# Opening of a two-block transformer kernel: a new order of VectorE's and ScalarE's work, with weight splits and their fetches moved

## The reference

```python
# 1. the modulation of block 1: six rows of 1024 from one conditioning vector
mod_x = silu(c) @ mod_w + mod_b             # 48 tiles of 128 outputs, 1024 inputs each
sh1, sc1, g1, sh2, sc2, g2 = split(mod_x, 6)
# 2. the pooling mixer of block 1, its residual and its norm
hx = x * (1 + sc1) + sh1
p  = [centred_window_mean(hx_g, w) - hx_g  for g, w in enumerate((2, 4, 8, 16))]
ox = einsum('blgc,gcd->blgd', p, pool_w) * pool_scale
x  = layer_norm(2**0.25 * x + g1 * ox)      # its input to the feed-forward: x * (1 + sc2) + sh2
# 3. the long filters of block 2's Hyena mixer, and their spectra
h  = sin(freq * (sin(freq * (sin(...)) @ fw2 + fb2)) @ fw3 + fb3) @ fw_out
k_f = rfft(two_sided_kernel(h_fwd * decay, h_bwd * decay))
```

## Time and profile before

| | us |
| --- | --- |
| median of 3 runs | 1805.95 |
| lowest, highest | 1804.77, 1806.22 |
| the profiled execution | 1806.09 |
| span of its profile | 1804.8 |

### The profile page before, as it was taken

One profiled execution on the slowest core, in us unless ns is written; L12 is line 12 of the kernel. 1 busy time (PEld: TensorE's weight loads), 2 busy tenths in 40 slices (PEclk: granted clock), 3 DMA queues, 4 the chain that ended last, 5 costly groups with the idle time before them and its releaser, 6 DMA issues.

```text
span 1804.8 us, 19463 instructions
## 1 busy us (share of the span) xinstructions
PE 1755.3 (97%) x7744; PEld 1399.1 (78%) x7744; DVE 950.4 (53%) x1360; ACT 621.2 (34%) x879; POOL 701.1 (39%) x321
## 2 busy tenths in 40 slices
PE   8999999999999999999999999999999999999996
PEld 4456888888887667788888888788888788888885
DVE  8787433321365875664444213687785754444124
ACT  2524222221244554243333213532233533333222
POOL 2112444444433021334444444365553344444442
PEclk9999999999999999999999999999999999999998
DMA  9873422332221020223223222522223233322321
GB/s 360 299 282 117 138 96 94 98 101 94 94 84 62 10 70 24 82 76 100 94 96 103 94 94 93 187 94 88 87 94 109 78 94 99 100 94 93 104 95 71
DMA packets 54538, 195.76 MB, mean 108 GB/s; under 512 B 6188, under 2 KB 7406, under 8 KB 52590
## 3 DMA queue, kind: packets, MB, share of 16 engines
q1 hardware_dynamic: 52781, 188.37, 31.0%
q10 hardware_dynamic: 1666, 6.14, 1.0%
HBM read 181.90 MB, written 12.58 MB: 108 GB/s over the span
## 4 chain that ended last, share of the span: by engine, by line
PE 84%; DVE 10%; POOL 2%; issue 2%; ACT 1%; DMA 1%; SPq 0%; DVEq 0%; ACTq 0%; POOLq 0%
PE ps L518 25%; PE ps L520 25%; PE ps L519 25%; PE ps L545 2%; PE ps L574 1%; PE ps L549 1%; DVE mod_ring L1775 1%; POOL w_lo L1610 1%; DVE softmax_stats L2144 1%; DVE filter_taps L1839 1%; PE ps L677 1%; DMA mod_ring<-in_mod_t 1%; PE ps L696 1%; PE ps L561 1%; PE ps L684 0%
## 5 line engine op out<-in xcount | busy, mean ns | idle before, releaser
L1610 POOL TENSOR_TENSOR w_lo<-w_raw,w_hi 128x1024 fp32r<-128x1024 f32 (+1 forms) x234 | 570.4, 2439 | 815.3 <-ACT w_hi L1119 740.4
L1119 ACT ACTIVATE w_hi<-w_raw 128x1024 fp32r<-128x1024 f32 (+1 forms) x238 | 251.3, 1056 | 791.7 <-PE ps L520 760.3
L518 PE MATMUL ps<-act_hi,w_hi 128*128 128x512 f32 x1240 | 485.9, 392 | 5.7 <-DVE x_residual L1861 3.0
L520 PE MATMUL ps<-act_hi,w_lo 128*128 128x512 f32 x1240 | 483.2, 390 | 0.0
L519 PE MATMUL ps<-act_lo,w_hi 128*128 128x512 f32 x1240 | 483.0, 390 | 0.0
L518 PEld LDWEIGHTS ps<-act_hi,w_hi 128*128 128x128 f32 x1240 | 233.0, 188 | 55.4 <-DVE x_residual L1861 3.4
L520 PEld LDWEIGHTS ps<-act_hi,w_lo 128*128 128x128 f32 x1240 | 233.0, 188 | 48.8
L519 PEld LDWEIGHTS ps<-act_lo,w_hi 128*128 128x128 f32 x1240 | 233.1, 188 | 48.5 <-issue 0.7
L518 PE MATMUL ps<-f_hidden_hi,w_hi 128*128 128x512 f32 x528 | 208.2, 394 | 0.0
L520 PE MATMUL ps<-f_hidden_hi,w_lo 128*128 128x512 f32 x528 | 207.4, 393 | 0.0
L519 PE MATMUL ps<-f_hidden_lo,w_hi 128*128 128x512 f32 x528 | 205.6, 389 | 0.0
(11 more groups left out here) (307 smaller groups left out, 2470.4 us busy)
## 6 DMA issues: line engine op xcount, KB each, us to landing
w_raw<-in_w_stream SPq DMA_DIRECT2D x250, 512.0 KB, 3.4
mod_ring<-in_mod_t SPq DMA_DIRECT2D x18, 512.0 KB, 11.4
x_tokens<-in_mod_t SPq DMA_DIRECT2D x18, 512.0 KB, 9.6
spectra<-filter_spectra SPq DMA_DIRECT2D x16, 512.0 KB, 8.3
hy_filter<-spectra SPq DMA_DIRECT2D x8, 1024.0 KB, 4.8
mod_ring_more<-in_mod_t SPq DMA_DIRECT2D x12, 512.0 KB, 11.5
x_residual<-in_xT ACTq DMA_DIRECT2D x8, 256.0 KB, 11.8
x_tokens<-in_x_tokens SPq DMA_DIRECT2D x1, 2048.0 KB, 13.3
```

Source lines behind the costliest of these rows:

```text
L518: PE.matmul(o, lh, rh, start=start, stop=False, **kw)
L520: return PE.matmul(o, ll, rh, start=False, stop=stop, **kw)
L1119: SC.activation(B.weights(c)[0][:, 0:n], B.WR[:, c % 2, 0:n], ACT.Copy).then_inc(S.w_hi, 1)
L1610: GP.tensor_tensor(low[:, 0:n], B.WR[:, c % 2, 0:n], f32(high[:, 0:n]), ALU.subtract).then_inc(S.w_lo, 1)
```

## The change

TensorE's order stays. The four others get new orders in the opening:

- **SyncE** fetches all nine first modulation tiles ahead of weight chunk 0, and chunk 1 only behind the stores of unit 0's spectrum.
- **ScalarE** splits chunk 1 behind `copies(0)` and takes `copies(2)` ahead of `pool_in`; the copies of unit 3 are laced into `pool_in` where those of unit 2 were, and the scaling of the residual stands behind them. In the norm the squares and the copies of unit 6 are laced anew.
- **VectorE** takes decays and butterflies earlier and row sums later, cuts the pooled tiles into pairs, moves `butterfly(6)` into the sums of squares, and row sums 37 to 39 behind them (`difference_low` is the same subtraction under a name).
- **GpSimd** takes the low parts at other points, by other semaphores.

```diff
@@ ScalarE, scalar_program.start @@
         w_hi(0)
+        copies(0)
         w_hi(1)
-        copies(0)
         copies(1)
+        copies(2)
         SC.wait_ge(S.x_in, 16 * KD)
         SC.wait_ge(S.affine, 1)
         SC.wait_ge(S.fw_sums, 2)
-        pool_in(0, 2)
-        even_part(2, 0)
-        pool_in(2, 4)
-        even_part(2, 1)
-        pool_in(4, KD)
-        plus_part(2, 0)
-        plus_part(2, 1)
+        pool_in(0, 3)
+        even_part(3, 0)
+        pool_in(3, 5)
+        even_part(3, 1)
+        pool_in(5, KD)
+        plus_part(3, 0)
+        plus_part(3, 1)
         for k in range(KD):
             SC.activation(X[:, k, :], X[:, k, :], ACT.Copy, scale=ALPHA_1).then_inc(S.x_scaled, 1)
-        copies(3)
...
-        even_part(6, 0)
         SC.wait_ge(S.decayed, 32)
         w_hi(4)
+        first_square(0)
+        even_part(6, 0)
+        first_square(1)
+        first_square(2)
         even_part(6, 1)
-        first_square(0)
-        first_square(1)
+        first_square(3)
+        first_square(4)
         plus_part(6, 0)
-        first_square(2)
-        first_square(3)
+        first_square(5)
         plus_part(6, 1)
-        for k in range(4, KD):
-            first_square(k)
+        first_square(6)
+        first_square(7)
@@ GpSimd, gpsimd_program.start @@
-        GP.wait_ge(S.mod_used, 5)
+        GP.wait_ge(S.mod_used, 9)
         w_lo(0)
-        GP.wait_ge(S.mod_used, 11)
+        GP.wait_ge(S.mod_used, 13)
         w_lo(1)
...
-        GP.wait_ge(S.mod_used, 31)
+        GP.wait_ge(S.diff_lo, 8)
         w_lo(2)
-        GP.wait_ge(S.mod_used, 37)
+        GP.wait_ge(S.mod_used, 32)
         w_lo(3)
-        GP.wait_ge(S.mod_used, 40)
+        GP.wait_ge(S.ln_centred, 1)
         w_lo(4)
         GP.wait_ge(S.ln_stat, 1)
         power(0).then_inc(S.ln_power, 1)
+        GP.wait_ge(S.ln_scaled, 1)
         w_lo(5)
@@ VectorE, vector_program.start @@
         decays(1)
         mod_tiles(4, 9)
+        decays(2)
         butterfly(0)
-        mod_tiles(9, 11)
-        decays(2)
-        mod_tiles(11, 15)
+        mod_tiles(9, 12)
         butterfly(1)
-        mod_tiles(15, 16)
+        mod_tiles(12, 13)
         decays(3)
-        mod_tiles(16, 20)
+        mod_tiles(13, 16)
         butterfly(2)
+        mod_tiles(16, 19)
         decays(4)
-        mod_tiles(20, 21)
+        mod_tiles(19, 21)
         for k in range(KD):
             difference(k)
         butterfly(3)
-        mod_tiles(21, 24)
+        mod_tiles(21, 22)
         decays(5)
-        mod_tiles(24, 29)
+        mod_tiles(22, 26)
+        pooled_tile(0)
+        pooled_tile(1)
         butterfly(4)
-        for m in range(4):
-            pooled_tile(m)
-        mod_tiles(29, 31)
+        pooled_tile(2)
+        pooled_tile(3)
+        mod_tiles(26, 28)
         for k in range(4, KD):
-            VE.wait_ge(S.diff_hi, k + 1)
-            VE.tensor_tensor(AL[:, k - 4, :], B.hx[:, k, :], f32(AH[:, k - 4, :]),
-                             ALU.subtract).then_inc(S.diff_lo, 1)
+            difference_low(k)
         decays(6)
-        mod_tiles(31, 33)
-        for m in range(4, KD):
-            pooled_tile(m)
+        mod_tiles(28, 30)
+        pooled_tile(4)
+        pooled_tile(5)
         butterfly(5)
-        mod_tiles(33, 37)
+        pooled_tile(6)
+        pooled_tile(7)
+        mod_tiles(30, 32)
         decays(7)
-        mod_tiles(37, MOD_LATE)
+        mod_tiles(32, 37)
         VE.wait_ge(S.ln_mean, 1)
...
+            if k == 4:
+                butterfly(6)
-        butterfly(6)
+        mod_tiles(37, 38)
         VE.wait_ge(S.ln_turned, 1)
         VE.tensor_scalar(B.stat[:, 0, :], ps[:, 7, 0:4], EPS_1, None, ALU.add).then_inc(S.ln_stat, 1)
+        mod_tiles(38, MOD_LATE)
         norm(0, lambda: butterfly(7))
@@ SyncE, sync_program @@
-    modulation(0, 6)
-    fetches(0, 2)
-    modulation(6, every)
+    modulation(0, every)
+    fetch(0)
     SP.dma_start(B.ident[:, :], a["identity"]).then_inc(S.ident_in, 16)
     modulation(every, every + MOD_OWN)
     spectrum_out(0)
+    fetch(1)
     modulation(14, 16)
```

More of the change, by code:

```diff
@@ L1880, in start, with difference_low @@
             mod_tiles(q, q + 1)
+        def difference_low(k):
+            VE.wait_ge(S.diff_hi, k + 1)
+            VE.tensor_tensor(AL[:, k - 4, :], B.hx[:, k, :], f32(AH[:, k - 4, :]),
+                             ALU.subtract).then_inc(S.diff_lo, 1)
         decays(1)
         mod_tiles(4, 9)
+        decays(2)
         butterfly(0)
-        mod_tiles(9, 11)
-        decays(2)
-        mod_tiles(11, 15)
+        mod_tiles(9, 12)
         butterfly(1)
-        mod_tiles(15, 16)
+        mod_tiles(12, 13)
         decays(3)
-        mod_tiles(16, 20)
+        mod_tiles(13, 16)
         butterfly(2)
+        mod_tiles(16, 19)
         decays(4)
-        mod_tiles(20, 21)
+        mod_tiles(19, 21)
         for k in range(KD):
```

## The result

| | us |
| --- | --- |
| before, median of 4 runs | 1806.09 |
| after, median of 4 runs | 1818.36 (1815.94 to 1818.9) |
| after over before | 1.0068, 95% interval 1.0056 to 1.0081 |
| the profiled execution of after, and its span | 1818.9, 1817.6 |

The changed kernel is 12.3 us slower, where 1807.2 was forecast with 1802.5 to 1812.5 as its range. The forecast was wrong, and on the slower side. Rival (b) came true, with 4.3 us; the larger part of the miss lies ahead of it.

The account below looks back on a forecast made before the run. The opening was taken to bound the kernel, by when the first feed-forward matmul starts (148.01 before). Terms +6.4 -5.1 -2.3 +1.3 +0.9 = +1.2 us put it at 149.2 and the time at 1807.2, range 1802.5 to 1812.5.

Parts of the forecast that it names:

- Rival (b): Before the windows: second decay table lands last, at U+21.1, first difference 4.2 us late plus 1.8 for clock, 1813.2; chance 0.15.
- `act_lo` term: At the first norm: GpSimd's last low part blocks VectorE's `act_lo`, so it ends late, +0.9 us (bounds 0 and 0.9).
- stop A: TensorE in unit 0, near 31.5: waits 3.4 us for ScalarE's first even copy behind chunk 0's split, plus 1.3 for clock.
- stop B: TensorE in unit 1, near 46.5: waits 5.8 us for the copy behind chunk 1's split, plus 1.7 to 2.4 for clock.
- the 4.18 us stop: TensorE's wait before 56.47 for ScalarE's even copies of unit 2 behind `pool_in`; claimed to go, with 1.8 us of clock.
- U: Time at which unit 1 ends on TensorE: forecast 57.8 us, bounds 56.1 and 59.7, against 45.3 before.
- the pooled-tile stop: TensorE's wait before 96.39 for VectorE's first pooled tile; claimed to go, -2.97 us and -2.1 for clock and issue.
- VectorE comes 0.9 us behind the mean: At the first norm: VectorE, with fewer row sums ahead, is 0.9 us late instead of 3.2, a gain of 2.3.
- the transform behind the column sums stays slow: At the norm: the transform at 141.80 takes 3.49 us; full clock would give 1.7, a gain of 1.2, taken as 0.
- those of 118.2: Earlier two stores and a chunk into an empty queue: chunk 1.0 us behind the first store, landing 5.0 later, 6.0 in all.
- tie at the windows: Before the windows: `decays(4)` and two row sums end at U+21.7, `difference(0)` can start at U+21.65; priced at 0.
- signs of being wrong: In the later profile: chunk 1 before 48 or no second stop; windows before 74 or after 81; `DMA decay` ending VectorE's wait.

## Why the prediction was wrong, step by step

**Held.** That the time is set by the feed-forward's start: the stretch behind it moved by 1.0 us, and that is the `act_lo` term. That stop A and stop B come, why, and behind which transfer. That the 4.18 us stop goes, that from U on nothing is late until the windows (U+20.6 = 83.38, as measured), that the pooled-tile stop goes (-4.9 against -5.1), that VectorE comes 0.9 us behind the mean (0.98), and that the transform behind the column sums stays slow. Also the block at the norm: `act_lo` and GpSimd's low part in the kernel after,

```profile
159.74 2.23 DVE L1971 SCALAR_TENSOR_TENSOR act_lo<-n_values,affine,act_hi 128x512 fp32r<-128x512 f32 x1
```
```profile
159.03 2.40 POOL L1612 TENSOR_TENSOR w_lo_extra<-w_raw,w_hi_extra 128x1024 fp32r<-128x1024 f32 x1 [3.14 <-DVE n_values L1966]
```

0.74 us when alone, 2.23 beside it, and the second k tile 0.95 late against 0.9. By the Trainium skill, page "SBUF — State Buffer", "Who interferes with whom", that is the lock on the shared read port; the trace agrees, and with the low part moved away the 2.23 is gone.

**Failed: the size of U (5.0 us in this profile).** The step "Unit 1 ends at U = 57.8 (bounds 56.1 and 59.7)"; it was 62.78. The forecast saw that `butterfly(0)` stands behind taps(2), so the issue was right (5.8 us behind unit 0's end, measured 5.9). Three sizes weren't. "0 to 2.6 for the clock; I take 1.3" at stop A: from 35.47 to 42.01 eight pieces took 6.54 us for 3.43, so 3.1, outside the bounds. With 0.6 for chunk 0, which landed at 33.88 and not 33.3, that makes the stores 2.5 us late. "Two stores and a chunk land like those of 118.2 ... 5.0 later": 7.0 here and 5.7 to 5.9 in four other profiles of this order. In the earlier trace rows nothing came behind it; here the tiles of three row sums and 2 MB of tokens are issued within 3.1 us behind chunk 1. And 2.8 instead of 2.1 for the clock behind stop B. The profiled execution is on the long side: U less the start of unit 0 is 35.8 in it and 30.8 to 35.1 in three kernels with the same front, where the forecast had 29.7. In the two shortest of them U is 58.87 and 59.30, inside the forecast's bounds, and chunk 0 landed anywhere from 33.2 to 38.0 in the nine profiles with its late fetch. So the bounds were too narrow for one execution, and how much of the 5.0 belongs to the kernel at its median stays open.

**Failed: the tie at the windows (4.3 us), rival (b).** "It lands at about U+17 ... A tie, priced at 0." VectorE's wait for it ended at U+19.9: the table was issued 1.3 us later than worked out and took 9.6 us to land instead of 8.1, above the 8 us from which (b) was to decide. The mechanism and its point were both written down; what was wrong was to price at 0 a chain with nothing in hand (U+21.7 against U+21.65 by the forecast's own sum) and give its loss 0.15. The first difference came at 87.35, U+24.6. Of the forecast's own signs of being wrong, both came: windows after 81, and `DMA decay` at the end of VectorE's wait.

**Failed: unit 5 (2.5 us in this profile; the run without it is 7 faster by the medians, which isn't explained).** No step of the prediction has it. It followed the row sums that the change moves back on VectorE, but not the queue that waits for them: their slots, the fetches into them, and chunk 2 behind those in the same order. The stop is 1.9 to 3.8 us in every kernel with the new orders and the old place of `fetches(2, 4)`, early front or late.

**What the change is worth without its transfers.** The new orders with the chunks put back are level with before: 6.7 us won ahead of the windows, 9.8 lost in them, 4.8 won behind, 3.0 lost in unit 5, 2.5 won from the mean to the first matmul of the feed-forward, and 0.8 lost right behind it to `act_lo`. With the table in time, `decays(4)` laced and chunks 2 and 3 in time as well the kernel is 5.5 us faster than before.

## What to carry to other kernels

When an order on an engine is changed, follow each moved instruction into the queue that waits for it: what slot it frees, which fetch fills that slot, and what is fetched behind. Two moves that cost nothing or little alone can meet in one chain, so try them together and apart. A tie in the sum is not a zero: with transfers on one side it is the likeliest place of a loss, and the repair to try is to bring the fetch forward or to put the waiting instruction behind those that need nothing. A repair can show nothing until the next stop is repaired too, as with the decay table here.

## What the runs showed of the hardware

- A chunk of 512 KB behind two stores of the same size landed 4.5 to 4.7 us from its issue where the stores were issued 2 us apart, and 5.7 to 7.0 where stores and chunk were issued within 1 us and 3.5 MB came behind them. With stores and chunk close together and nothing behind, it was 5.0. What comes behind isn't all of it: in the kernel before with the moved fetches alone, 3 MB were issued within 2.3 us behind the chunk and it landed in 4.7. How the two share the delay stays open.
- What a stop costs in clock, by the eight pieces behind it (3.43 us at 2.4 GHz), isn't set by its length: 3.1 us behind a stop of 4.86, 1.8 behind 3.43, 2.8 behind 7.51, 1.6 behind 6.22, and 1.6, 1.9 and 3.2 behind three stops of 6.44. Behind stops of 1.0 to 1.2 us, and of 1.9 to 2.8 in unit 5, the pieces were at full clock; behind 2.6 in the windows they were not.
